# Experts' lead given to block 1, four blocks of 64 slots, and a tail that folds a gain into its weights

## What is computed

```
h += mixer(RMSNorm(h))          # gated conv and window attention
m  = RMSNorm(h)
logits = m @ w_router + b_router; top 4 of 32 experts per token
for each expert: act = swiglu(m[its tokens] @ w_up[e] + b_up[e])   # w_up 1024 x 2048
                 y   = act @ w_down[e] + b_down[e]                 # w_down 1024 x 1024
h += sum of gate * y over the token's 4 experts
h += sigmoid(RMSNorm(h; g_ple) @ w_ple_gate) * (p @ w_ple)
out = RMSNorm(h; g_final)
```

## Time and profile before

| | |
|---|---|
| median of 3 runs | 1496.08 us (1495.47 to 1502.73) |
| the profiled execution | 1496.07 us, of it 1494.2 us span |
| mean granted TensorE clock | 0.992 |
| PE busy | 1463.3 us (98%) |
| DVE, ACT, POOL busy | 733.3, 246.4, 99.4 us |
| DMA moved | 492.14 MB |
| first expert matmul to the end of the last down | 389.8 to 1408.0 us |

### The profile page before, as it was taken

One profiled execution on the slowest core, in us unless ns is written; L12 is line 12 of the kernel. 1 busy time (PEld: TensorE's weight loads), 2 busy tenths in 40 slices (PEclk: granted clock), 3 DMA queues, 4 the chain that ended last, 5 costly groups with the idle time before them and its releaser, 6 DMA issues.

```text
span 1494.2 us, 36367 instructions
## 1 busy us (share of the span) xinstructions
PE 1463.3 (98%) x15688; PEld 816.3 (55%) x15688; DVE 733.3 (49%) x1643; ACT 246.4 (16%) x449; POOL 99.4 (7%) x130
## 2 busy tenths in 40 slices
PE   9999999999999999999999999999999999999987
PEld 8999999987543334333344333344333344333575
DVE  5468333354655444543354543354543454545685
ACT  5433322224100000000000000000000000001236
POOL 0000000000000001000001000001000001000050
PEclk9999999999999999999999999999999999999999
DMA  8421922356999999999999999999999999999861
GB/s 285 146 63 52 324 87 86 110 190 246 342 375 405 413 414 413 404 410 416 415 414 415 405 407 415 414 415 412 401 410 411 413 412 411 399 408 411 342 215 47
DMA packets 57305, 492.14 MB, mean 329 GB/s; under 512 B 11079, under 2 KB 16439, under 8 KB 27300
## 3 DMA queue, kind: packets, MB, share of 16 engines
q1 hardware_dynamic: 50212, 473.59, 79.7%
q0 software_dynamic: 6928, 17.49, 3.3%
q10 hardware_dynamic: 96, 0.07, 0.0%
HBM read 478.28 MB, written 29.53 MB: 340 GB/s over the span
## 4 chain that ended last, share of the span: by engine, by line
PE 89%; DVE 4%; DMA 3%; ACT 2%; issue 1%; SPq 0%; DVEq 0%; ACTq 0%
PE ps L2494 41%; PE ps L2504 21%; PE ps L2088 11%; PE ps L2279 3%; DMA raw_pair<-w_up_pairs 3%; PE ps L2028 2%; PE ps L2030 2%; PE ps L2029 2%; PE ps L2491 2%; PE ps L2473 1%; ACT S L900 1%; DVE hq L1906 1%; DVE S L1316 1%; PE ps L2310 0%; PE ps L2659 0%
## 5 line engine op out<-in xcount | busy, mean ns | idle before, releaser
L2494 PE MATMUL ps<-raw_pair,xT 128*32 128x512 f32 x5688 | 620.6, 596 | 0.0
L2494 PEld LDWEIGHTS ps<-raw_pair,xT 128*32 128x32 f32 x5688 | 182.6, 111 | 422.3 <-issue 422.3
L2504 PE MATMUL ps<-raw_pair,acT 128*32 128x256 f32 x5760 | 316.3, 379 | 0.0
L2504 PEld LDWEIGHTS ps<-raw_pair,acT 128*32 128x32 f32 x5760 | 187.1, 110 | 135.9 <-issue 17.4
L1790 DVE TENSOR_SCALAR gl<-ps 128x256 f32<-128x256 f32 x94 | 34.2, 419 | 438.0 <-ACT gl L1094 438.0
L1832 DVE STREAM_TRANSPOSE acT<-arow 32x192 f32<-32x192 f32 (+1 forms) x512 | 187.1, 366 | 7.4
L1822 DVE STREAM_TRANSPOSE xT<-xg 32x256 f32<-32x256 f32 x372 | 161.8, 435 | 11.5 <-DMA xg<-m_rows,ius 5.8
L1094 ACT ACTIVATE gl<-ps 128x256 f32<-128x256 f32 x94 | 29.4, 384 | 651.2 <-PE ps L2494 623.9
L2088 PE MATMUL ps<-aTh,wh 128*128 128x272 f32 x512 | 107.3, 291 | 0.1
L2088 PE MATMUL ps<-aTh,wl 128*128 128x272 f32 x512 | 106.0, 289 | 0.0
L2088 PE MATMUL ps<-aTl,wh 128*128 128x272 f32 x512 | 105.7, 288 | 0.0
(11 more groups left out here) (436 smaller groups left out, 1215.0 us busy)
## 6 DMA issues: line engine op xcount, KB each, us to landing
raw_pair<-w_up_pairs SPq DMA_DIRECT2D x122, 2048.0 KB, 16.0
raw_pair<-w_down_pairs SPq DMA_DIRECT2D x60, 2048.0 KB, 17.1
raw_pair<-w_mix SPq DMA_DIRECT2D x25, 1024.0 KB, 5.2
raw_pair<-w_up_pairs SPq DMA_DIRECT2D x9, 1024.0 KB, 5.4
y_rows<-c_zero SPq DMA_DIRECT2D x4, 2176.0 KB, 21.6
raw_pair<-w_down_pairs SPq DMA_DIRECT2D x8, 1024.0 KB, 19.0
yk<-y_rows SPq DMA_DIRECT2D x8, 1024.0 KB, 8.4
raw_pair<-w_ple_chunks SPq DMA_DIRECT2D x4, 1024.0 KB, 21.9
```

Of the source, the lines that this page charges most:

```text
L2494: ins = mmul(ps[32 * j:32 * j + 32, b, :], xT[:, k, 32 * g:32 * g + 32], w[:, 512 * q:512 * q + 512], start=False, stop=(k == UPC - 1))
L2504: ins = mmul(ps[32 * j:32 * j + 32, bank + b, 0:LB], a, raw[slot][:, D * (k % 2) + LB * q:D * (k % 2) + LB * q + LB], start=(k == 0), stop ...
```

## The change

It has four parts. STASH becomes 1: block 1's chunks 0 to 2 go beside the ring, each loaded singly, chunk 1 after the router's logits and the others around the start of block 0. While block 0 runs, SP loads block 2's first pair into the ring slots 0 and 1 and block 1's chunk 3 into slot 3; block 2 skips its first pair, block 7 skips nothing. SMALL becomes (2, 3, 4, 5), PEEL 8. The gain g_ple goes out of the rows and into the weights: a tiny `gpc` [128, 8] replaces the 512 KB `gple` and `gpl4`, `round_ple` and `split_ple` scale by it in four pieces of 512 columns, PE turns `hq` itself. The order of SP's last loads changes: the last down chunks first, then bd3 and the gate chunks, the rows of tile 0 ahead of the last gate chunk. The first and second token tile are handled by halves, chunks of w_ple_gate have the column half fastest, and five filler matmuls (FILL1) follow the turn of tile 1.

```diff
-PEEL = 6
-SMALL = (2, 3)
+PEEL = 8
+SMALL = (2, 3, 4, 5)
-STASH = 7
+STASH = 1
+FILL1 = 5
...
+            sp.wait_ge(b_rnd, 2)
+            sp.wait_ge(lg_mm, NT)
+            sp.dma_start(ahead[1], one(w_up, STASH, 1)).then_inc(ahead_in, 16)
             sp.wait_ge(pp_mm, NT)
             sp.dma_start(raw[3][:], one(w_up, 0, 3)).then_inc(landed[3], 16)
+            sp.dma_start(ahead[0], one(w_up, STASH, 0)).then_inc(ahead_in, 16)
             sp.wait_ge(tab_done, 1)
-            sp.dma_start(ahead2[:], w_up[bass.ds(e_ahead, 1), 0].rearrange("e p n -> (e p) n")).then_inc(ahead_in, 16)
-            sp.dma_start(ahead[2][:], one(w_up, bass.ds(e_ahead, 1), 2)).then_inc(ahead_in, 16)
+            sp.dma_start(ahead[2][:], one(w_up, STASH, 2)).then_inc(ahead_in, 16)
...
-                    if stash and q == 0:
+                    if isinstance(i, int) and i == STASH + 1 and q == 0:
                         continue
                     sp.wait_ge(tiles_done, TB + l + 2 if first else TB + 12 * i - 16 + l + 2)
-                    if stash and q == 1:
-                        sp.dma_start(raw[3][:], one(w_up, bass.ds(e_cur, 1), 3)).then_inc(landed[3], 16)
+                    if first and q == 1:
+                        sp.dma_start(raw[3][:], one(w_up, STASH, 3)).then_inc(landed[3], 16)
                         continue
-                    if first:
-                        src = w_up[1, q]
+                    if first and q == 0:
+                        src = w_up[bass.ds(expert_of(STASH + 1), 1), 0].rearrange("e p n -> (e p) n")
+                    elif first:
+                        src = w_up[STASH, q]
...
+            for l in range(DNC):
+                sp.wait_ge(tiles_done, TB + 12 * nb - 16 + l + 1)
+                sp.dma_start(raw[l][:], one(w_dn, bass.ds(e_prev, 1), l)).then_inc(landed[l], 16)
             sp.wait_ge(xh_done, nb)
             for g in range(3):
                 sp.dma_start(bd3[NEXP * g:NEXP * g + NEXP].bitcast(F32), bs_dram[:, g % 2, 2 * FF:]).then_inc(bd_in, 16)
-            sp.dma_start(gple[:], A["g_ple_rows"]).then_inc(gf_in, 16)
...
-                nc.scalar.activation(gate_h[g - 1][:], gate_r[g - 1][:], ACT.Copy).then_inc(rounded, 1)
+                act.wait_ge(gf_in, 16)
+                for j in range(KH):
+                    cols, k = slice(512 * j, 512 * j + 512), KH * ((g - 1) // 2) + j
+                    ins = nc.scalar.activation(gate_h[g - 1][:, cols], gate_r[g - 1][:, cols], ACT.Copy, scale=gpc[:, k:k + 1])
+                ins.then_inc(rounded, 1)
...
-                nc.vector.tensor_tensor(gate_l[g - 1][:], gate_r[g - 1][:], gate_h[g - 1][:].bitcast(F32), ALU.subtract)\
-                  .then_inc(split_done, 1)
+                for j in range(KH):
+                    cols, k = slice(512 * j, 512 * j + 512), KH * ((g - 1) // 2) + j
+                    ins = nc.vector.scalar_tensor_tensor(out=gate_l[g - 1][:, cols], in0=gate_r[g - 1][:, cols], scalar=gpc[:, k:k + 1],
+                                                         in1=gate_h[g - 1][:, cols].bitcast(F32), op0=ALU.mult, op1=ALU.subtract)
+                ins.then_inc(split_done, 1)
...
-            add_rows(0)
+            add_half(0, (0, 1))
+            add_half(1, (0, 1))
+            add_half(0, (2, 3))
+            h_half_of(0)
...
-                    ins = nc.tensor.transpose(slot2(2)[:, P * k:P * k + P], xnb[:, i % 3, P * k:P * k + P], ident[:])
+                    ins = nc.tensor.transpose(slot2(2)[:, P * k:P * k + P], hq[i][:, P * k:P * k + P], ident[:])
+                ins.then_inc(ntr, 1)
+                if i == 1:
+                    for _ in range(FILL1):
+                        mmul(ps[:, 2 * GATE_SLOT[1], :], gT3[:, 0:P], bd3[:, 0:512], start=True, stop=True)
...
+                    if i == 0 and g == 0:
+                        n_turn_half(1)
+                    if at_g == (1 if i else 3) and i + 1 < NT:
```

More of the change, by code:

```diff
@@ L706, in _ @@
             tile_rows(0)
+            sp.wait_ge(tiles_done, TB + 12 * nb - 7)
+            sp.dma_start(gate_r[3][:], A["w_ple_chunks"][4]).then_inc(landed[8], 16)
             sp.wait_ge(tiles_done, TB + 12 * nb)
@@ L1203, in out_std, with n_high_half @@
                 nc.scalar.activation(stdt[:, 1, i:i + 1], src, ACT.Sqrt, scale=1.0 / D, bias=epsb[:, 0:1]).then_inc(std_out, 1)
+            def n_high_half(i, hf):
+                act.wait_ge(ntr, 2 * i + hf + 1)
+                nc.scalar.activation(nTh[:, i, 4 * hf:4 * hf + 4].rearrange("p k n -> p (k n)"), ps[:, 4 + hf, :], ACT.Copy)\
+                  .then_inc(nhi if hf else nhi_half, 1)
             def n_high(i):
-                if i == 0:
-                    for hf in range(2):
-                        act.wait_ge(ntr, hf + 1)
-                        nc.scalar.activation(nTh[:, 0, 4 * hf:4 * hf + 4].rearrange("p k n -> p (k n)"), ps[:, 4 + hf, :], ACT.Copy)\
-                          .then_inc(nhi if hf else nhi_half, 1)
-                    return
-                act.wait_ge(ntr, i + 2)
+                act.wait_ge(ntr, i + 3)
                 if i < NT - 1:
@@ L1896, in add_rows @@
                 y = yk[i % 2] if i < NT - 1 else yk4
-                for k in range(0, TOPK, 1 if i == 0 else 2):
-                    if i:
-                        dve.wait_ge(pair_sum, 2 * (i - 1) + k // 2 + 1)
-                    elif k == 0:
-                        dve.wait_ge(x_in[0], 48)
-                    elif k == 2:
-                        dve.wait_ge(y_in, 16)
+                for k in range(0, TOPK, 2):
+                    dve.wait_ge(pair_sum, 2 * (i - 1) + k // 2 + 1)
                     if k:
@@ L1907, in add_rows, with add_half, h_half_of @@
                     added[0] += 1
+            def add_half(hf, planes):
+                cols = slice(512 * hf, 512 * hf + 512)
+                for k in planes:
+                    dve.wait_ge(*((x_in[0], 48) if k < 2 else (y_in, 16)))
+                    if k:
+                        dve.wait_ge(y_add, added[0])
+                    nc.vector.tensor_tensor(hq[0][:, cols], hq[0][:, cols], yk[0][:, k, cols], ALU.add).then_inc(y_add, 1)
+                    added[0] += 1
+            def h_half_of(hf):
+                cols = slice(512 * hf, 512 * hf + 512)
+                dve.wait_ge(y_add, added[0])
+                dve.wait_ge(bd_mm, hf + 1)
+                nc.vector.tensor_tensor(hq[0][:, cols], ps[:, 2 * BIAS_SLOT[0] + hf, :], hq[0][:, cols], ALU.add)\
+                  .then_inc(h_add if hf else h_half, 1)
             dve.wait_ge(tiles_done, TB + 12 * nb)
@@ L2565, in body @@
                     else:
-                        up_chunk(l, xT1 if first else xT, ahead[l] if stash and l < 3 else raw[l])
+                        up_chunk(l, xT1 if first else xT, ahead[l] if first and l < 3 else raw[l])
                 pe.wait_ge(ah_done, i)
@@ L2669, in gates_of @@
                     pe.wait_ge(g_sig, 2 * (i - 1))
-                for g in range(4):
+                for at_g, g in enumerate((0, 2, 1, 3) if i else range(4)):
                     if i == 0:
@@ L2744 @@
     ple = [a["w_ple"][0].reshape(2, P, D).transpose(1, 0, 2).reshape(P, CH)]
-    ple += [quarter(a["w_ple_gate"][0], kh, ch) for ch in range(2) for kh in range(2)]
+    ple += [quarter(a["w_ple_gate"][0], kh, ch) for kh in range(2) for ch in range(2)]
     arrays["w_ple_chunks"] = np.ascontiguousarray(np.stack(ple))
@@ L2750 @@
         a["w_down"][0].reshape(NEXP, DNC // 2, 4, P, D).transpose(0, 1, 3, 2, 4).reshape(NEXP, DNC // 2, P, 2 * CH))
[L2751 removed]
+    arrays["g_ple_cols"] = np.ascontiguousarray(a["g_ple"].reshape(KT, P).T)
     arrays["g_final_rows"] = np.ascontiguousarray(np.tile(a["g_final"].reshape(1, D), (P, 1)))
```

160 lines of the change are left out of this document (65 added, 95 removed).

## The result

The kernel after takes **1508.26 us** (median of 6 runs, 1503.58 to 1509.91); the kernel before, run beside it, 1496.22 (6 runs). The ratio is 1.0067, 95% interval 1.005 to 1.0084: about 10 us slower. I had forecast 1499 with a range to 1507; the ratio times 1496 gives 1506, just inside, while the median of 1508.26 lies outside. A second series gave 1507.02 and again 1.0067. The profiled execution took 1509.53 us, its span is 1507.7, its mean granted clock 0.989 (before: span 1494.2, 0.992).

What follows compares the result with a forecast made beforehand. Loads were taken as the bound, 32.2 us a block against PE's 32.0. A later yl (+5.1) and the gates (-2.1) made +3.0 us on 1496.07: 1499 us, range 1491 to 1507.

Steps and rivals of the forecast that it cites:

- the side that I gave 0.24: Whole kernel: the chance given to a slower result; same had 0.64, faster 0.12.
- the early chunk: Routing, before block 0 ends: block 1's chunk loads in idle DMA time beside block 0's gather; 0, at most +1 us.
- the sum: Whole kernel: +5.1 for the later yl and -2.1 at the gates, +3.0 us on 1496.07, so 1499 us.
- The clock as a rival: Last two blocks and before first gates: PE's landing waits lower its clock, 1506 us; chance 0.23, shared with full lead loss.
- The lead: Ring, lead moved from block 7 to block 1: later landings +7.3 us, less 2 regained, so +5.3.
- 2 of 5.2 regained: Ring from block 2: a queue entering empty could catch up 0 to 5.2 us of backlog; 2 was taken.
- The small blocks: Expert phase: two more small blocks take 20.3 us from PE and nothing from the loads; 0 us booked.
- The last block: Block 30's second down pair lands 1.2 us after PE wants it; the last down ends at 1409.2, +1.2.
- The landing of the gate chunks: Tail: the third gate chunk lands at 1410.0, from 1405.9 plus 5.3 (late landings) minus 1.2 (fewer bytes).
- From the gate chunk to `yl`: Tail: scaled rounding 2.5 us and split 2.8 until 1415.3, only then yn and yl; yl +5.1 us.
- The gates: Gate stage: the 3.33 us wait ahead of tile 1's turn goes, -3.3; five fillers +1.2; sum -2.1 us.
- if the wait only moves to the low part of a half: Gate stage: condition under which the gates' gain would be 0 instead of -2.1 us.

Runs made afterwards that it cites:

- late_load: Kernel after, with block 1's chunk 1 issued behind block 0's last chunk instead of during the routing: 1502.74 us, ratio 1.0031.
- early_alone: Kernel before, with only block 1's second chunk (one megabyte) also loaded early, as in the change: 1502.26 us, ratio 1.0027.
- small2: Kernel after, with two small blocks (2, 3) instead of four: 1505.3 us, ratio 1.0059.
- stash7: Kernel after, with the three chunks beside the ring given back to block 7; four small blocks and new tail kept: 1497.13 us, ratio 0.9997.
- tail_alone: Kernel after, with the lead at block 7 and two small blocks as before, so the new tail alone: 1498.22 us, ratio 1.0.
- refill: late_load, with the three buffers beside the ring filled a second time, for block 7, which skips those chunks in the ring: 1498.94 us, ratio 1.0009.
- late_latesplit: late_load, with rounding and splits of gate chunks 2 and 3 behind yh and yl, and tile 0's first low part earlier: 1505.03 us, ratio 1.0062.
- Stash7_latesplit: stash7, with the rounding and split of gate chunk 3 alone moved behind yh and yl: 1501.01 us, ratio 1.0026.

## Why the prediction came out as it did

**The result** is on the side that I gave 0.24. The forecast of 1499 was 7 to 9 us too low. That 1506, by the ratio, still lies within 1491 to 1507 is luck: the upper end was made of nothing regained of the lead and of a clock loss in the last two blocks and ahead of the gates, and the greater part of the miss came from a term that the range hardly held, the early chunk with its "at most +1". For the kernel without the early megabyte the ratio is 1.0031 (1.002 to 1.0042); the sum (+3.0 us, 1.002) lies at the lower edge of that.

**The early chunk: the step that failed.** "It shares the engines with block 0's gather: 0, at most +1." late_load gives 5.5 us for it, early_alone about 5 at the median (1502.26 for 1497.07, 4.0 by its ratio of 1.0027, with the extra read in it). I had priced the megabyte as bytes in idle time and had not asked when PE needs the gather. In the trace of before the rows landed at 387.0 (issued 381.5, 5.5 to landing), and PE turned them at 387.05: **no slack at all**. A load of 14.7 us beside it makes the gather 2.5 us longer, and PE stands for it. In some executions the clock then falls to 0.50 for some 6 us, which cost 3.0 us in the kernel after. The Trainium skill says in "DMA: Bandwidth & Descriptors", section "Issuing engines are not separate DMA queues", that transfers from different queues run on the same 16 engines and interleave; the gather, issued by POOL against a load of SP, agrees with it (8.0 us for 5.5). The idle engines of that stretch (a share of 0.26 from 384 to 388 before) were not free capacity: with them full the gather landed too late.

**The clock as a rival: right in kind, wrong in place.** I had put it in the last two blocks and before the gates, fed by waits for landings. Those waits came (19 of them, 24.4 us, between 425 and 700 us, the longest 2.6), and the clock did dip there: 0.92 from 540 to 550, 0.96 from 480 to 560. In the last blocks it did not (1.00 from 1330 to 1408). Small2, with 6.4 us of such waits, is not clear of the kernel after, so the dips cost little that can be measured, PE waiting for loads anyway; and no run shows the "one wait of 2 us a block" from which I let this rival decide. What it did cost came from the start. The Trainium skill, "TensorE: Matmul & The Clock Gate", section "HAM oscillation — how this bites in real kernels", describes a kernel in which a wait for a DMA ahead of every tile lets the next tile begin cold; its waits are longer than these. Here the work behind a wait of 2.37 and 2.42 us began at the lower clock, and that behind 2.45 and 2.64 us did not.

**The lead: right.** +5.3 forecast, 5.6 (5.1 by the ratios) measured between late_load and stash7, and the idle window is there. How it came about is less clean: between block 30's down pair of stash7 (landed 1384.4) and of late_load (1392.4) lie 8.0 us, 0.6 of it from the start of block 0: all of the 7.3 and none of the 2 regained. But the tail of stash7 gives part of its gain away. So the "2 of 5.2 regained" was not seen, and that the time came out near +5.3 is in part luck.

**The small blocks: right.** 0 of 20.3, shown alone (1.0006) and, to within 3 us, inside the change.

**The last block: right.** The last down of late_load ends at 1410.95; forecast 1409.2, and its start had slipped by 1.1.

**The landing of the gate chunks: mis-sized by 3.1 us.** I had let the third gate chunk gain 1.2 us on block 30's second down pair, for the bytes that no longer stand between them. In the kernel before it lands 18.4 us behind that pair (1405.9 for 1387.5). In every kernel with the new order of the last loads it lands later behind it, not sooner: 20.3 us in the kernel after (1419.5 for 1399.2), 19.8 in small2, 20.9 in tail_alone, 19.7 in refill. Fewer bytes took longer, though the engines are not full there: their share falls from 0.84 to 0.13 between 1406 and 1418 in the kernel after. In the kernel before it falls as well, from 0.60 to 0.16 between 1402 and 1408. What holds back the last bytes of these chunks stays open.

**From the gate chunk to `yl`: right.** The chain of landing, rounding, split and `yn` was to take 5.3 us; in the kernel after `yn` begins at 1424.94, 5.4 behind the landing at 1419.5. The second chunk lands 2.7 us ahead of the third, before it was 3.0, and its rounding (2.56) and split (2.7) just fit in between, so the rows of ACT and DVE show eight pieces in one. In late_load `yl` came 8.4 us later than before, where +5.1 was forecast; 3.1 of the 3.3 too much are the landing.

**The gates: half.** -2.1 forecast. The five fillers took 1.41 us for the 1.2 forecast. From `yl`'s start to the last gate stage it is 67.1 us before (1411.78 to 1478.87), 65.5 in late_load and 65.9 after, so -1.2 to -1.6; in tail_alone, where little else waits, 68.2, and the time shows no gain (ratio 1.0). The wait of 3.33 us did go. I had named the danger, "if the wait only moves to the low part of a half", as a bound of 0, and tail_alone says that the sum should have stood there.

**The sum, term by term.** In the trace of the kernel after, +13.5 us stand against +3.0: the start 7.2 for 0, from there to the last down 2.6 for 1.2, from there to `yl` 4.9 for 3.9, the gates -1.2 for -2.1. By the runs' ratios the early megabyte is 5.4 us, the place of the lead 5.1, and what is left of the change (stash7) -0.4, together the 10 us of the kernel after; they add up by construction, since each kernel is compared with the next. No version here beats the kernel before; stash7 equals it.

**Two readings in the prediction.** The slices 13 to 37 of the earlier trace rows run from 399 to 416 GB/s, not from 402; nothing rests on it. And the prediction sets its 431 GB/s against a figure for both cores of a pair; this kernel runs on one core, so its trace does not speak against that figure.

## What to carry to other kernels

Before a load is put into idle DMA time, look up which small, late transfer runs in that stretch and how much slack its reader has: idle engines may be what keeps a gather just in time. A lead is worth the idle time that it fills, wherever it lies; once the ring runs at its ceiling, work taken from PE only turns into waits. Fewer bytes ahead of a load need not make it land sooner. And where a wait of PE falls may matter as much as its length: with the clock at 0.50 under the gate products of late_latesplit that stretch took 9.6 us, for 6.5 with the clock back at 1.00 in late_load. That is one pair of traces, not a test by itself.

## What I had not expected of the hardware

- After waits of nearly the same length, in the same place, the clock fell to 0.50 for some 6 us (2.37 and 2.42 us) or did not fall (2.45 and 2.64 us). One kernel has runs of 1504 and of 1511 us, and this is part of the reason (a run of 1507.78 at a mean clock of 0.993 is not explained by it). What decides is open.
- The fourth chunk's split took far longer beside POOL. DVE's timeline of the kernel after:

```profile
1438.85 2.10 DVE L1878 SCALAR_TENSOR_TENSOR gate_l<-raw_pair,gpc,gate_h 128x512 fp32r<-128x512 f32 x1 [1.17 <-ACT gate_h L1141]
```

The first of its four pieces takes 2.10 us, where eight took 5.39 at 1419.52, 0.67 each; POOL adds two planes of `yk` at that time, from 1435.66 to 1440.40. The three pieces behind it take 2.0 us together. The Trainium skill, "GPSIMD Engine Reference", section "8. Key points", says that GpSimd shares its SBUF interfaces with VectorE and names instructions with two SBUF inputs; this one has two, and the row agrees. Stash7_latesplit has both cases side by side: the split at 1426.42, with POOL busy up to 1428.0, took 4.12 us, the next at 1431.06, with POOL idle, 2.73. That it is POOL was not tried by itself.
- ACT's rounding of a gate chunk takes 2.56 us in four scaled pieces, 1.91 in one plain instruction: cutting it by columns and scaling it costs 0.65 us a chunk, and it stands in the chain of the tail.
